# In the attention stage of a hybrid decoder step, ScalarE empties every second PSUM bank of transposed probabilities and VectorE the others

## The chip, the core and the metric

The kernel runs on one core of a Trainium2 chip. The metric is the time of one execution on the device in microseconds (us). The engines of a core that this text speaks of are TensorE (PE in the profile, PEld for its weight loads), VectorE (DVE), ScalarE (ACT), GpSimd (POOL) and SyncE (SP, which issues DMAs). Each works through its own list of instructions in order; they meet at semaphores.

## What is computed

One inference step of a two-layer decoder over a prompt of 1024 positions and eight sample sequences of 8 new positions each, model width 1024, all in float32. Layer 0 mixes tokens by retention and a gated recurrence; layer 1 by attention with 16 heads of 64 over three dilated windows. Both layers end in a SwiGLU block. The change lies in the attention of layer 1, whose prompt part is, for each pattern:

```
s = jnp.einsum('znqhd,znkhd->znhqk', qb, kc) * (Dh ** -0.5)
...
s = s - alibi_slopes()[:, None, None] * (d * diff)
s = jnp.where(valid[:, None], s, -jnp.inf)
m = jnp.max(s, axis=-1, keepdims=True)
p = jnp.exp(s - m)
den = jnp.sum(p, axis=-1)
o = jnp.einsum('znhqk,znkhd->znqhd', p, vc) / den.transpose(0, 1, 3, 2)[..., None]
```

The three patterns' results are then combined by their softmax denominators. The kernel folds the three patterns into one softmax over all earlier keys with a table of biases, which gives the same sum. The sample part does the same for 8 queries of each of eight sequences against a cache of 2048 keys and values, gathered by stride.

## The kernel before

Attention is done in 64 **steps**, one for each pair of heads and each block of 128 queries: step n has pair n // 8 and query block n % 8. The eight steps of a pair are called its first to eighth step; the eighth has eight key blocks (W = 1024), the first has one. A step's probabilities are worked on in three successive steps. For the pair's two heads (e = 0, 1) the stages are:

- `scores(n)` on TensorE (line 1833), into PSUM banks 0 to 3. VectorE adds the bias and takes the row extreme (line 2071, into `att_scores`), ScalarE does the exponentials in place with their sums (`probs(n, 0)` and `probs(n, 1)`, line 1982).
- In step n + 1 TensorE transposes these probabilities, 128x128 block by block (`turn`, line 1869), four blocks to a PSUM bank. Each bankful is a **unit** `("p", n, c)`, where c is its first block: 0, 4, 8, 12. An engine copies it to SBUF as `att_pt` (`take`, line 2036 on VectorE). A step of query block q has 2(q + 1) blocks, so one unit for q = 0 and 1, two for 2 and 3, three for 4 and 5, four for 6 and 7.
- In step n + 2 TensorE multiplies `att_pt` with the values (`pv`, line 1911) and spreads the inverse denominators (line 1915); ScalarE copies those out (`att_rden_rows`, line 2009), VectorE multiplies (`att_out`, line 2105).

All transposes share two PSUM banks (4 and 5) in turns: unit number g goes to bank g % 2, and `turn` first waits until unit g - 2 has been taken. `turns(n)` writes out by hand what units a step has. In steps up to 58 the sample work is woven in: three or four units of transposed cache keys (`"k"`, taken by ScalarE, `smp_kt`, line 1965) stand ahead of the "p" units in six of eight steps; in the other two stand units of queries and keys of the next pair ("qk") and of sample probabilities ("s"). A unit list of an eighth step is k, k, k, p0, p4, p8, p12. TensorE places units 0 and 1 first, then `pv` of step n - 2, then units 2 and 3, then the rest, with sample work between.

From step 59 on no cache keys are left, so the "p" units stand first: the **tail**. Step 61 has two units "out" ahead of them. Steps 64 and 65 have no scores of their own; step 65 has only `pv(63)`. After it comes the output projection (line 223), fed by `att_hi` (ScalarE, line 1815) and `att_lo` (VectorE, line 1819).

ScalarE's order within a step is set by these lines, where `mine` are the units that it takes:

```
for i in mine[0:2]:
    take(n, i)
...
if 0 <= n < NSLOT:
    probs(n, 0)
for i in mine[2:3]:
    take(n, i)
if 0 <= n < NSLOT:
    probs(n, 1)
for i in mine[3:]:
    take(n, i)
```

After them comes line 2009. At the end of step 61 ScalarE also splits a weight block (`w_hi`, line 205), and VectorE its rest (`w_lo`, line 209) at the end of step 62. VectorE does in each step: the scores' extremes (2071), a reciprocal (2076), its takes, then 2105.

Of the kernel before, what the change touches and what calls it, by code (L numbers as in the profile page):

```python
# [18 lines left out]
ACT = mybir.ActivationFunctionType  # L19
AX = mybir.AxisListType  # L20

P = 128
# [3 lines left out]
QT = SEQ // P  # L26
# [104 lines left out]
def build(nc, a):  # L131
# [349 lines left out]
    w = O_WORK  # L481
# [4 lines left out]
    w = O_WORK + 9 * TA  # L486
# [11 lines left out]
    w = O_X  # L498
# [22 lines left out]
    w = O_WORK  # L521
# [1153 lines left out]
    w = O_X  # L1675
# [5 lines left out]
    w = O_HL  # L1681
    BI = at("att_bias", w, [P, 2, 2, SEQ])
    PT = at("att_pt", w + 16384, [P, 2, 2 * QT, P])
# [12 lines left out]
    w = O_WORK  # L1696
# [48 lines left out]
    def turns(n):  # L1745
# [16 lines left out]
            units += [("s", b, z) for z in range(3)]  # L1762
        return units

    T0 = {}
    nt = 0
    for n in SLOTS:
# [3 lines left out]
    def last_turn(n, what, x):  # L1771

        g = T0[n] + max(i for i, u in enumerate(turns(n)) if u[0] == what and u[1] == x)
        return g % 2, g // 2 + 1

    def k_last(b, t):
        s = max(i for i in range(8) if K_AT[i] <= 2 * t + 1)
# [43 lines left out]
    def s9_pe(pe):  # L1821
# [78 lines left out]

        def pv(m):
            p, qb = divmod(m, QT)
            bank, count = last_turn(m + 1, "p", m)
            pe.wait_ge(t_out[bank], count)
            if qb == 0:
                pe.wait_ge(a_vl[p % 2], 16 * (p // 2 + 1))
            if m:
                pe.wait_ge(a_ox, m)
            for x in range(qb + 1):
                for e in range(2):  # L1910
                    pe.matmul(PS[e * DH:(e + 1) * DH, 6, 0:P], VN[p % 2][:, x, e * DH:(e + 1) * DH],  # L1911
                              PT[:, m % 2, e * (qb + 1) + x, :], start=(x == 0), stop=(x == qb), tile_position=(0, e * DH))
            pe.wait_ge(a_dg, m + 1)
            for e in range(2):
                mm = pe.matmul(PS[e * DH:(e + 1) * DH, 6, P:2 * P], ones[:, 0:DH], ADG[:, m % 2, e, :],
                               start=True, stop=True, tile_position=(0, e * DH))
            mm.then_inc(a_o, 1)
# [37 lines left out]
    def s9_act(act):  # L1955
        def take(n, i):
            what, x, c = turns(n)[i]
            g = T0[n] + i
            bank = PS[:, 4 + g % 2, :]
            act.wait_ge(t_in[g % 2], g // 2 + 1)  # L1960
            if what in ("qs", "ks"):
                act.activation((QTS, KTN)[what == "ks"][:, :, :].rearrange("p a w -> p (a w)"), bank,
                               ACT.Copy).then_inc(t_out[g % 2], 1)
            elif what == "k":
                act.activation(SKT[:, x % 2, 4 * c:4 * c + 4, :].rearrange("p a w -> p (a w)"), bank,  # L1965
                               ACT.Copy).then_inc(t_out[g % 2], 1)
            elif what == "qk":
                t = (QH, KH)[c // 2][x % 2]
                act.activation(t[:, (c % 2) * 512:(c % 2 + 1) * 512], bank, ACT.Copy).then_inc(q_hi, 1)
            else:  # L1970
                for e in range(2):
                    r = slice(e * DH, (e + 1) * DH)
                    dst = OX[r, :, S0 + 4 * x * DS:S0 + (4 * x + 4) * DS].rearrange("p k (b q) -> p b k q", q=DS)
                    src = bank[r, :].rearrange("p (b k e q) -> p b k e q", b=4, e=2, q=DS)[:, :, :, e, :]
                    op = act.activation(dst, src, ACT.Copy)
                op.then_inc(t_out[g % 2], 1)
# [8 lines left out]
        act.wait_ge(v_park, 16)  # L1985
        for n in SLOTS:
            b, s = sample_slot(n)
            mine = [i for i, u in enumerate(turns(n)) if u[0] not in ("p", "s")]
            for i in mine[0:2]:
                take(n, i)  # L1990
            if s == 6:
                act.wait_ge(b_mn, b + 1)
                act.activation(SS[:, :], SS[:, :], ACT.Exp, bias=NMN[:, 0:1], scale=-1.0,
                               accum_out=DNS[:, 0:1]).then_inc(b_p, 1)
# [8 lines that stand above are left out]
            if n == NSLOT + 1:  # L2003
                act.wait_ge(a_red, 2 * NSLOT)
                for k in range(3):
                    out1_hi(act, k)
            if 2 <= n:
                act.wait_ge(a_o, n - 1)
                act.activation(RS[:, n % 2, :], PS[:, 6, P:2 * P], ACT.Copy).then_inc(a_rc, 1)
            if n == NSLOT - LEAD + 1:  # L2010
                act.wait_ge(b_oc, DB)
                for e in range(2):
                    act.activation(ODUP[:, :, e, :], OALL[:, :].rearrange("p (b d) -> p b d", b=DB),
                                   ACT.Copy).then_inc(b_du, 1)
            if n == NSLOT - 3:
                split_hi(act, B_OUT1, B_OUT1 % RING)

    def s9_dve(dve):
# [41 lines left out]
        for n in SLOTS:  # L2060
# [19 lines left out]
                weigh(DB - 1)  # L2080
            for f in range(1, 5):
                for i in range(2 * f - 2, min(2 * f, len(units)) if f < 4 else len(units)):
                    if units[i][0] in ("qk", "p", "s"):
                        take(n, i)
                for t in SCORED.get((s, f), ()):
                    if t % 2:
# [296 lines left out]
```

## Time and profile before

| what | value |
|---|---|
| median of 3 runs | 2931.81 us (2929.42 to 2933.04) |
| profiled execution | 2934.2 us |
| its span from first to last instruction | 2932.4 us |
| PE busy | 2860.6 us, 98% of the span |
| DVE busy | 1358.0 us, 46% |
| ACT busy | 782.8 us, 27% |

The span is cut into engine busy times; the profiled execution's own time is 1.8 us above its span. Busy times are means over stages with different limits: the attention stage, from about 1562 to 2031 us of the span, has to be read by itself. A timeline row gives the start, the length, the engine, the line and operation, how many instructions were merged (x8), and in brackets the idle time of the engine ahead of it with what ended it.

### The profile page before, as it was taken

What the parts mean: (1) busy time and instruction counts of PE and PEld (TensorE: products, weight loads), DVE (VectorE), ACT (ScalarE), POOL (GpSimd) and SP (SyncE); (2) the same over time, 40 slices, a digit from 0 to 9 for tenths busy, and PEclk for the clock granted to TensorE, in tenths of its full rate; (3) what the DMA queues carried; (4) which work ended last, traced back from release to release, by engine and by line L of the source; (5) the groups of instructions that cost most, each with busy time, mean ns of one, the idle gap of its engine ahead of it and who ended that gap; (6) DMA issues with size and microseconds to landing.
All of it is one profiled execution on the core that took longest, in us unless ns stands there. A gap on an engine that the chain in (4) does not pass through costs nothing.

```text
span 2932.4 us, 47539 instructions
## 1 busy us (share of the span) xinstructions
PE 2860.6 (98%) x21361; PEld 2721.7 (93%) x21361; DVE 1358.0 (46%) x1756; ACT 782.8 (27%) x1238; POOL 117.4 (4%) x218
## 2 busy tenths in 40 slices
PE   7999999999999999999998999998999999999999
PEld 6999999999999999999996766777999999999999
DVE  5754544444444444745403555556444444444444
ACT  5443522111111111322215444444221111111111
POOL 1010000000000000000001111110000000000000
PEclk9999999999999999999999999999999999999999
DMA  5120211111111111222338667763111111111111
GB/s 190 44 67 18 105 58 44 44 44 44 44 44 44 44 44 44 105 75 90 102 122 275 203 202 248 247 196 123 58 44 44 44 44 44 44 44 44 44 44 61
DMA packets 126249, 253.80 MB, mean 87 GB/s; under 512 B 7585, under 2 KB 88693, under 8 KB 125536
## 3 DMA queue, kind: packets, MB, share of 16 engines
q1 hardware_dynamic: 112960, 189.29, 20.0%
q0 software_dynamic: 11776, 56.96, 5.7%
q10 hardware_dynamic: 1312, 4.52, 0.4%
q8 instruction: 169, 2.77, 0.4%
q14 instruction: 32, 0.26, 0.0%
HBM read 222.72 MB, written 28.02 MB: 86 GB/s over the span
## 4 chain that ended last, share of the span: by engine, by line
PE 91%; DVE 3%; ACT 3%; DMA 2%; SPq 1%; issue 1%; POOL 0%; ACTq 0%; POOLq 0%; DVEq 0%
PE psum L223 63%; PE psum L459 14%; PE psum L1854 3%; PE psum L1911 2%; PE psum L1869 2%; PE psum L1833 2%; PE psum L1882 1%; ACT smp_kt L1965 1%; DMA cache_tile<-in_cache_k 1%; SPq L1804 1%; DMA x_natural<-in_x_prompt 1%; PE psum L1935 0%; DVE att_pt L2036 0%; PE psum L568 0%; ACT att_scores L1982 0%
## 5 line engine op out<-in xcount | busy, mean ns | idle before, releaser
L223 PE MATMUL psum<-h_hi,w_hi 128*128 128x364 f32 (+1 forms) x2592 | 574.9, 330 | 6.5 <-DVE h_lo L289 5.6
L223 PE MATMUL psum<-h_lo,w_hi 128*128 128x364 f32 (+1 forms) x2592 | 571.6, 329 | 0.0
L223 PE MATMUL psum<-h_hi,w_lo 128*128 128x364 f32 (+1 forms) x2592 | 568.7, 328 | 0.0
L223 PEld LDWEIGHTS psum<-h_hi,w_hi 128*128 128x128 f32 x2592 | 448.6, 188 | 10.0 <-issue 6.8
L223 PEld LDWEIGHTS psum<-h_lo,w_hi 128*128 128x128 f32 x2592 | 449.1, 188 | 0.0
L223 PEld LDWEIGHTS psum<-h_hi,w_lo 128*128 128x128 f32 x2592 | 449.0, 188 | 0.0
L205 ACT ACTIVATE w_hi<-w_raw 128x2048 fp32r<-128x2048 f32 x96 | 183.5, 1912 | 665.5 <-PE psum L223 609.1
L459 PE MATMUL psum<-w_hi,h_hi 128*128 128x256 f32 (+1 forms) x1152 | 325.8, 283 | 0.0
L459 PE MATMUL psum<-w_hi,h_lo 128*128 128x256 f32 (+1 forms) x1152 | 323.6, 281 | 0.0
L459 PE MATMUL psum<-w_lo,h_hi 128*128 128x256 f32 (+1 forms) x1152 | 322.9, 280 | 0.0
L1473 DVE TENSOR_TENSOR x_res<-x_res,psum 128x1092 f32<-128x1092 f32 x176 | 227.3, 1292 | 200.3 <-PE psum L223 200.3
L209 DVE TENSOR_TENSOR w_lo<-w_raw,w_hi 128x2048 fp32r<-128x2048 f32 x96 | 219.6, 2288 | 63.2 <-ACT w_hi L205 49.0
L223 PE MATMUL psum<-ffn_hi,w_hi 128*128 128x364 f32 (+1 forms) x1056 | 233.3, 329 | 0.0
L223 PE MATMUL psum<-ffn_lo,w_hi 128*128 128x364 f32 (+1 forms) x1056 | 232.8, 328 | 0.0
L223 PE MATMUL psum<-ffn_hi,w_lo 128*128 128x364 f32 (+1 forms) x1056 | 232.7, 328 | 0.0
L459 PEld LDWEIGHTS psum<-w_hi,h_hi 128*128 128x128 f32 (+1 forms) x1152 | 215.1, 187 | 2.1 <-issue 1.2
L459 PEld LDWEIGHTS psum<-w_lo,h_hi 128*128 128x128 f32 (+1 forms) x1152 | 215.2, 187 | 0.0
L459 PEld LDWEIGHTS psum<-w_hi,h_lo 128*128 128x128 f32 (+1 forms) x1152 | 215.0, 187 | 0.0
L1450 DVE TENSOR_TENSOR ffn_t<-psum,rstd 128x1092 f32<-128x1092 f32 x44 | 57.0, 1296 | 296.7 <-PE psum L223 296.7
L1459 DVE TENSOR_TENSOR ffn_t<-psum,rstd 128x1092 f32<-128x1092 f32 x44 | 57.0, 1296 | 278.8 <-PE psum L223 278.6
L1422 ACT ACTIVATE ffn_hi<-ffn_t 128x1092 fp32r<-128x1092 f32 x44 | 49.2, 1118 | 507.6 <-DVE ffn_t L1461 507.6
L223 PEld LDWEIGHTS psum<-ffn_lo,w_hi 128*128 128x128 f32 x1056 | 183.0, 188 | 0.0
(309 smaller groups left out, 3192.5 us busy)
## 6 DMA issues: line engine op xcount, KB each, us to landing
cache_tile<-in_cache_k SPq DMA_DIRECT2D x64, 512.0 KB, 8.2
cache_tile<-in_cache_v SPq DMA_DIRECT2D x64, 512.0 KB, 5.6
w_raw<-in_w_ffn_gate SPq DMA_DIRECT2D x22, 1024.0 KB, 5.1
w_raw<-in_w_ffn_up SPq DMA_DIRECT2D x22, 1024.0 KB, 5.1
w_raw<-in_w_ffn_down SPq DMA_DIRECT2D x22, 1024.0 KB, 4.9
w_raw<-in_w_in_att SPq DMA_DIRECT2D x12, 1024.0 KB, 7.1
w_raw<-in_w_in_rec SPq DMA_DIRECT2D x10, 1024.0 KB, 5.0
park_x<-x_res POOLq DMA_DIRECT2D x2, 4368.0 KB, 14.0
```

Source lines behind the costliest of these rows:

```text
L205: act.activation(WHI[:, slot, :], RAW[:, :], ACT.Copy).then_inc(wh_done, 1)
L209: dve.tensor_tensor(WLO[:, slot, :], RAW[:, :], WHI[:, slot, :].bitcast(F32), ALU.subtract).then_inc(wl_done, 1)
L223: mm = pe.matmul(PS[:, bank + c, 0:n], st[:, slot, wc:wc + P], mv[:, k, c * CW:c * CW + n], start=(i < NCH), stop=(i >= 3 * NCH * nk - NCH))
L459: mm = pe.matmul(PS[0:n, bank, 0:BW], st[:, k, w:w + n], mv[:, slot, k * BW:(k + 1) * BW], start=(k == 0 and x == 0) if used is None else ...
L1422: act.activation(GH[:, par, f, :], TG[:, :], ACT.Copy).then_inc(fgh, 1)
L1450: i = dve.tensor_tensor(v3(TG[:, :]), PS[:, 0:3, 0:CW], r3, ALU.mult)
L1459: dve.tensor_tensor(v3(TG[:, :]), PS[:, 3:6, 0:CW], r3, ALU.mult).then_inc(fch, 1)
L1473: dve.tensor_tensor(x, x, PS[:, b0:b0 + 3, 0:CW], ALU.add).then_inc((a_out, b_out)[m % 2], 1)
L1833: mm = pe.matmul(PS[:, 2 * e + c // 512, 0:min(512, W - c)], q[p % 2][e * DH:(e + 1) * DH, qb * P:(qb + 1) * P], k[p % 2][e * DH:(e + 1) * ...
L1854: mm = pe.transpose(to[:, h * P:(h + 1) * P], TILE[j % 8][:, hp * P:(hp + 1) * P], ident[:, :])
L1869: mm = pe.transpose(to[:, (k - c) * P:(k - c + 1) * P], SX[x % 2][:, e, y * P:(y + 1) * P], ident[:, :])
L1911: pe.matmul(PS[e * DH:(e + 1) * DH, 6, 0:P], VN[p % 2][:, x, e * DH:(e + 1) * DH], PT[:, m % 2, e * (qb + 1) + x, :], start=(x == 0), stop ...
```

## The change

Of each step's "p" units, ScalarE now takes the second (c = 4) and the fourth (c = 12); VectorE keeps c = 0 and c = 8. TensorE's `pv` now waits for the last two units, since two engines may take them, where before it waited for the last one.

```
+    def by_act(unit):
+        what, x, c = unit
+        return c % 8 == 4 if what == "p" else what != "s"
...
+    def last_turns(n, what, x):
+
+        gs = [T0[n] + i for i, u in enumerate(turns(n)) if u[0] == what and u[1] == x]
+        return [(g % 2, g // 2 + 1) for g in gs[-2:]]
...
-            bank, count = last_turn(m + 1, "p", m)
-            pe.wait_ge(t_out[bank], count)
+            for bank, count in last_turns(m + 1, "p", m):
+                pe.wait_ge(t_out[bank], count)
...
+            elif what == "p":
+                k = min(4, 2 * (x % QT + 1) - c)
+                act.activation(PT[:, x % 2, c:c + k, :].rearrange("p a w -> p (a w)"), bank[:, 0:k * P],
+                               ACT.Copy).then_inc(t_out[g % 2], 1)
...
-            mine = [i for i, u in enumerate(turns(n)) if u[0] not in ("p", "s")]
+            mine = [i for i, u in enumerate(turns(n)) if by_act(u)]
...
-                    if units[i][0] in ("qk", "p", "s"):
+                    if units[i][0] == "qk" or not by_act(units[i]):
```

The first place is ScalarE in an eighth step (W = 1024), with the line of the exponentials at 1982 before and 1995 after. Before:

```order
L1965 ACTIVATE smp_kt<-psum 128x512 x2
L1982 ACTIVATE att_scores_176,att_den<-att_scores_176,att_max 128x1024
L1965 ACTIVATE smp_kt<-psum 128x512
L1982 ACTIVATE att_scores_176,att_den<-att_scores_176,att_max 128x1024
L2009 ACTIVATE att_rden_rows<-psum 128x128
```

With the change:

```order
L1974 ACTIVATE smp_kt<-psum 128x512 x2
L1995 ACTIVATE att_scores_176,att_den<-att_scores_176,att_max 128x1024
L1974 ACTIVATE smp_kt<-psum 128x512
L1995 ACTIVATE att_scores_176,att_den<-att_scores_176,att_max 128x1024
L1978 ACTIVATE att_pt<-psum 128x512
L1978 ACTIVATE att_pt<-psum 128x256
L2022 ACTIVATE att_rden_rows<-psum 128x128
```

Two copies have come in between the second exponential and the copy of the inverse denominators.

The second place is ScalarE in the tail, from step 61's exponentials (128x768) to the end of step 63. Before:

```order
L1982 ACTIVATE att_scores_176,att_den<-att_scores_176,att_max 128x768 x2
L2009 ACTIVATE att_rden_rows<-psum 128x128
L205 ACTIVATE w_hi<-w_raw 128x2048
L1982 ACTIVATE att_scores_175,att_den<-att_scores_175,att_max 128x896 x2
L2009 ACTIVATE att_rden_rows<-psum 128x128
L1982 ACTIVATE att_scores_176,att_den<-att_scores_176,att_max 128x1024 x2
L2009 ACTIVATE att_rden_rows<-psum 128x128 x2
```

With the change:

```order
L1995 ACTIVATE att_scores_176,att_den<-att_scores_176,att_max 128x768
L1978 ACTIVATE att_pt<-psum 128x512
L1995 ACTIVATE att_scores_176,att_den<-att_scores_176,att_max 128x768
L2022 ACTIVATE att_rden_rows<-psum 128x128
L205 ACTIVATE w_hi<-w_raw 128x2048
L1978 ACTIVATE att_pt<-psum 128x512
L1995 ACTIVATE att_scores_175,att_den<-att_scores_175,att_max 128x896 x2
L2022 ACTIVATE att_rden_rows<-psum 128x128
L1978 ACTIVATE att_pt<-psum 128x512
L1978 ACTIVATE att_pt<-psum 128x256
L1995 ACTIVATE att_scores_176,att_den<-att_scores_176,att_max 128x1024 x2
L2022 ACTIVATE att_rden_rows<-psum 128x128
```

Here the copies of `att_pt` stand among and ahead of the exponentials: one between the two of step 61, one ahead of those of step 62 (128x896), two ahead of those of step 63 (128x1024).

The third place is TensorE in step 63 after its scores: the transposes of its first two units (`att_scores_175`), `pv(61)`, and the transposes of the third and fourth unit, with the semaphores that each waits for. It stands in the same order before and after; this is the kernel with the change:

```order
L1878 MATMUL psum<-ident,att_scores_175 128x128 [waits att_probs,att_taken0]
L1878 MATMUL psum<-ident,att_scores_175 128x128 x3
L1878 MATMUL psum<-ident,att_scores_175 128x128 [waits att_probs,att_taken1]
L1878 MATMUL psum<-ident,att_scores_175 128x128 x3
L1920 MATMUL psum<-att_pt,att_v_186 64x128 [waits att_out_done,att_taken1,att_taken0]
L1920 MATMUL psum<-att_pt,att_v_186 64x128 x11
L1924 MATMUL psum<-att_diag,ones 64x128 [waits att_diag]
L1924 MATMUL psum<-att_diag,ones 64x128
L1878 MATMUL psum<-ident,att_scores_175 128x128 [waits att_probs,att_taken0]
L1878 MATMUL psum<-ident,att_scores_175 128x128 x3
L1878 MATMUL psum<-ident,att_scores_175 128x128 [waits att_probs,att_taken1]
L1878 MATMUL psum<-ident,att_scores_175 128x128
```

Before, the first five of these rows are

```order
L1869 MATMUL psum<-ident,att_scores_175 128x128 [waits att_probs,att_taken0]
L1869 MATMUL psum<-ident,att_scores_175 128x128 x3
L1869 MATMUL psum<-ident,att_scores_175 128x128 [waits att_probs,att_taken1]
L1869 MATMUL psum<-ident,att_scores_175 128x128 x3
L1911 MATMUL psum<-att_pt,att_v_186 64x128 [waits att_out_done,att_taken1]
```

Nothing moved on TensorE; only the wait of `pv` grew by one semaphore. The third unit of step 63 and the fourth (two blocks) are placed after `pv(61)`, on both kernels.

## Rows read from the trace of the kernel before

**Rows 1.** Windows: us, busy (x) of each engine, granted clock, DMA share.

```profile
1740.00:1800.00 60.00, 56.32 (x716) 41.82 (x716) 33.67 (x95) 29.39 (x70) 9.86 (x18) 1.00 0.70 222
...
2018.00:2022.00 4.00, 1.75 (x19) 1.09 (x16) 3.85 (x9) 2.55 (x5) 0.61 (x1) 1.00 0.87 302
...
2022.00:2026.00 4.00, 4.00 (x36) 3.67 (x37) 1.79 (x5) 0.00 (x0) 0.61 (x1) 0.57 0.15 52
```

**Rows 2.** Groups by form, attention stage: busy us, mean ns, idle before.

```profile
L2036 DVE COPY att_pt<-psum 128x512 f32<-128x512 f32 x128 | 86.0, 689 | 104.5 <-PE psum L1869 103.2
...
L2036 DVE COPY att_pt<-psum 128x256 f32<-128x256 f32 x32 | 13.5, 421 | 6.2 <-PE psum L1869 6.0
...
L1965 ACT ACTIVATE smp_kt<-psum 128x512 f32<-128x512 f32 x148 | 83.4, 595 | 154.8 <-PE psum L1854 154.4
...
L1982 ACT ACT_TABLE_LOAD x1 | 1.3, 1283 | 0.0
```

**Rows 3.** Line 1869, attention stage: TensorE's idle time before it (us, times).

```profile
  ACT smp_kt L1965: 22.9, 56
...
  DVE att_pt L2036: 14.6, 25
```

**Rows 4.** Timeline of the eighth step of a pair.

```profile
1736.74 1.14 ACT L1982 ACTIVATE att_scores<-att_scores,att_max 128x1024 f32<-128x1024 f32 x1
...
1737.15 1.09 PE L1869 MATMUL psum<-ident,att_scores 128*128 128x128 f32 x8
...
1737.85 1.65 DVE L2036 COPY att_pt<-psum 128x512 f32<-128x512 f32 x3
...
1737.87 0.27 ACT L2009 ACTIVATE att_rden_rows<-psum 128x128 f32<-128x128 f32 x1
...
1738.59 0.20 PEld L1869 LDWEIGHTS psum<-ident,att_scores 128*128 128x128 f32 x2 [0.58 <-DVE att_pt L2036]
```

**Rows 5.** Timeline of the steps after that.

```profile
1740.46 1.75 PE L1911 MATMUL psum<-att_pt,att_v 128*64 128x128 f32 x28
...
1757.34 0.20 PEld L1911 LDWEIGHTS psum<-att_pt,att_v 128*64 128x64 f32 x4 [0.17 <-issue]
```

**Rows 6.** Timeline of the tail, steps 60 to 62.

```profile
2000.90 1.09 PE L1869 MATMUL psum<-ident,att_scores 128*128 128x128 f32 x8 [0.34 <-DVE att_pt L2036]
...
2002.14 0.83 ACT L1982 ACTIVATE att_scores<-att_scores,att_max 128x640 f32<-128x640 f32 x1 [1.92 <-DVE att_max L2071]
...
2005.22 1.06 PE L1862 MATMUL psum<-ident,smp_out_twice 128*128 128x128 f32 x8 [0.95 <-ACT smp_out_twice L2013]
...
2009.61 1.91 ACT L205 ACTIVATE w_hi<-w_raw 128x2048 fp32r<-128x2048 f32 x1
...
2011.94 1.04 ACT L1982 ACTIVATE att_scores<-att_scores,att_max 128x896 f32<-128x896 f32 x1 [0.42 <-DVE att_max L2071]
...
2014.94 0.28 DVE L2105 TENSOR_TENSOR att_out<-psum,att_rden_rows 128x128 f32<-128x128 f32 x1
```

**Rows 7.** Timeline of the tail, steps 63 to 65.

```profile
2018.59 1.15 ACT L1982 ACTIVATE att_scores<-att_scores,att_max 128x1024 f32<-128x1024 f32 x1 [4.33 <-DVE att_max L2071]
...
2020.42 1.04 PE L1869 MATMUL psum<-ident,att_scores 128*128 128x128 f32 x6 [1.84 <-DVE att_pt L2036]
...
2021.87 1.79 PE L1869 MATMUL psum<-ident,att_scores 128*128 128x128 f32 x8 [0.41 <-DVE att_pt L2036]
...
2023.59 2.67 PE L1911 MATMUL psum<-att_pt,att_v 128*64 128x128 f32 x28
...
2026.40 1.09 PE L1869 MATMUL psum<-ident,att_scores 128*128 128x128 f32 x8
...
2028.73 1.97 PE L1911 MATMUL psum<-att_pt,att_v 128*64 128x128 f32 x32 [1.23 <-DVE att_out L2105]
```

**Rows 8.** Timeline of the output projection's start.

```profile
2036.27 3.10 ACT L1815 ACTIVATE att_hi<-att_out 128x1092 fp32r<-128x1092 f32 x3
...
2038.75 0.46 PEld L223 LDWEIGHTS psum<-att_hi,w_hi 128*128 128x128 f32 x3 [0.49 <-DVE att_lo L1819]
```

## The prediction

> **What bounds the kernel now.** I read the windows first, to see the attention stage by itself. In a middle stretch of it TensorE is busy 56.32 of 60 us, VectorE 33.67, ScalarE 29.39 [rows 1]: TensorE sets the pace and neither copying engine is full. What the change can win is therefore only idle time of TensorE that a copy of `att_pt` ends; what it can cost is idle time that it adds there. I next asked which waits end TensorE's idle time before the transposes of probabilities (line 1869). ScalarE's `smp_kt` ends 22.9 us of it, 56 times, VectorE's `att_pt` 14.6 us, 25 times, matmul and weight-load side added [rows 3]. Then I read the timeline of each kind of step. In the steps that carry cache keys, a transpose of probabilities waits for `att_pt` in one place only: the fourth unit (c = 12) of an eighth step waits for the bank of the second (c = 4), 0.58 us on the weight-load side [rows 4]. Seven eighth steps are of this kind (7, 15, ..., 55); the rest of the 14.6 us is in the tail. So two places have to be worked out: the eighth step, seven times, and the tail, once.
>
> **What moves.** Per pair the second units are one of 256 columns and five of 512, the fourth ones one of 256 and one of 512. That is 8 copies per pair, 64 in all, 48 of 512 columns and 16 of 256. VectorE is freed of 48 x 0.689 + 16 x 0.421 = 39.8 us [rows 2]. ScalarE's copy from PSUM of 512 columns takes 0.595 us [rows 2] and one of 128 columns 0.27 [rows 4]; on the line between them 256 columns take 0.38. ScalarE gains 48 x 0.595 + 16 x 0.38 = 34.6 us. Table loads are not added: copy and exponential already alternate on ScalarE with a single load in the stage [rows 2]. `pv` waits for one semaphore more in most steps. Today the first `pv` of a pair already waits for three (it adds the values' load), and its gap of 0.17 us [rows 5] is that of the others; I cost the wait at nothing (bounds 0 and 0.05 us x 50, 2.5 us).
>
> The Trainium skill, Perfetto Trace Analysis, Optimizing Scalar/DVE Operations, says that moving work to ScalarE may pay where VectorE is saturated. By that rule this change has nothing to win, since VectorE stands at 56% here.
>
> **The eighth step, with cache keys.** The first transposes of c = 4 are done some 0.65 us after 1737.15, and VectorE begins to copy them at 1737.85; the copy takes 0.69, and TensorE goes on at 1738.59, 0.05 us after its end [rows 4]. On ScalarE this copy stands behind the second exponential, which runs from 1736.74 for 1.14 us, to 1737.88 [rows 4]. So it runs from 1737.88 to 1738.47 and TensorE goes on at 1738.52: 0.07 us are saved, no more, and 7 x 0.07 = 0.5 us in all. If ScalarE were free in time, TensorE's own gap of 0.2 us would be left and 0.38 saved each time, 2.7 us: the lower bound. ScalarE's later row `att_rden_rows` (1737.87 before [rows 4]) moves behind both copies, to about 1739.4. VectorE's `att_out` and the `pv` behind it wait for it; that `pv` starts at 1740.46 [rows 5], one microsecond later than needed, which hides it. If that cover were gone, each 0.1 us uncovered in seven pairs would cost 0.7. In the third to seventh step the copy on ScalarE likewise stands behind the second exponential and ahead of the idle time before the next step's first cache keys (154.8 us of ScalarE's idle time end at `smp_kt` copies [rows 2], some 2 us at each step's first); nothing that TensorE waits for stands behind it. I take 0, bounds -2.7 and +2 us for the body without its 0.5.
>
> **The tail.** Here a step's "p" units are the first of `mine`, so ScalarE takes them ahead of its exponentials, and step by step falls behind. I follow it.
>
> Step 60: the transposes of both units run from 2000.90 for 1.09 us; the copy on ScalarE runs until about 2002.6, and the first exponential, 2002.14 before, starts 0.47 later [rows 6]. ScalarE stays late by that, and the "out" transposes, which waited for `smp_out_twice` at 2005.22 [rows 6], move by 0.47, with TensorE after them.
>
> Step 61: a copy stands between the two exponentials and waits 0.15 us for its transposes: 0.47 + 0.15 + 0.6 = 1.2 us late for the weight split, 2009.61 before and 1.91 long [rows 6]. It ends at 2012.7.
>
> Step 62: the copy of c = 4, 0.6 us, comes next; the exponentials, 2011.94 before [rows 6], start at 2013.3, 1.35 late. `att_rden_rows` follows them, and VectorE's `att_out` after it, before at 2014.94 [rows 6], at about 2015.66: 0.72 late. Behind it on VectorE stand the weight's rest and step 63's extremes, and behind these the take of step 63's first unit.
>
> Step 63: the third unit waits for that take and starts at 2020.42 + 0.73 = 2021.15; third and fourth are done 0.87 later, the 0.18 us that the fourth waited for VectorE in the 1.04 being gone [rows 7]: 2022.02. Only now can ScalarE copy the fourth unit, since it stands **ahead of the exponentials of step 63**: until 2022.44. Then two exponentials of 1.15 us [rows 7], with 0.1 us for the sum read between and behind: 2024.84, where before they had been over at about 2020.9. Step 64's first transposes read them. They start at 2024.89 instead of 2021.87 [rows 7]: **+3.0 us**.
>
> Step 64: before, the transposes took 1.79 us and `pv(62)` 2.67 [rows 7]; eight transposes at 2026.40 take 1.09 [rows 7] and 28 such matmuls elsewhere 1.75 [rows 5]. The granted clock was 0.57 between 2022 and 2026 (1.2 GHz for most of it), after a stretch of 4 us in which TensorE was busy 1.75 [rows 1]. With the change that stretch is emptier still, so I take the low clock to hold over the same work: 0 more. Bounds: full clock, -(0.70 + 0.92) = -1.6; the low clock over the next transposes and `pv(63)` too, +0.7 + 0.9 = +1.6, and over the first microseconds of the projection, some +1 more.
>
> The Trainium skill, TensorE: Matmul & The Clock Gate, HAM oscillation, holds that idle gaps on TensorE bring the low clock. By that rule a second gap after the first (2.9 us of idle time between 2022.0 and 2024.9) speaks for the bound above, not for the one below; the row before it agrees (0.57 after a gap of 1.84 us).
>
> End of step 64: the fourth unit is now copied by ScalarE (1.1 us after the transposes start, 0.6 long) ahead of `att_rden_rows`, and VectorE's `att_out` comes some 0.1 us later relative to the transposes; `pv(63)`, which waited 1.23 us for it at 2028.73 [rows 7], moves by that: **+0.1**. ScalarE's first three `att_hi`, which had filled the time of these transposes, begin 1.7 us later, so the chain `att_hi`, `att_lo`, `att_out(63)`, `att_hi` runs 1.3 us behind. Its last link was just in time: TensorE waited 0.49 us (0.19 of it felt) for the sixth `att_lo`, behind `att_hi` at 2036.27 [rows 8]. **+1.25 us** (bounds 0 and 1.7).
>
> **Sum.** -0.5 + 3.0 + 0 + 0.1 + 1.25 = +3.9 us. On the profiled execution's own 2934.2 us this gives 2938.1; that execution lies 2.4 us above the median of the runs, 2931.8, so the predicted time is 2935.7.
>
> **Rivals.** (1) *A gain*: VectorE's lighter queue lets extremes and `att_out` come sooner and TensorE loses its waits for `att_pt`. For it speak the 25 waits; against it that ScalarE is at its exponentials whenever a second unit is ready. It would give -2.7 in the body and up to -3 in the tail (VectorE is busy 3.85 of 4 us there [rows 1]): 2926 us. It decides if ScalarE's queue had 0.3 us to spare at the second units. Chance 0.06. (2) *A wash*: the tail's delay of the exponentials is made up, because VectorE reaches step 63 sooner by two copies (1.3 us) and `pv(62)` is not held: +3.0 shrinks to 1 or 2 and with full clock the sum is near 0: 2932 us. Chance 0.17. (3) *The stall feeds on itself*, slower by over 0.2%: the low clock lasts over `pv(63)` and the projection's start (+1.6 + 1), or the second copy of an eighth or first step holds `att_rden_rows` long enough that `pv` waits 0.3 us in 14 steps (+4). It decides once 2 us come on top of 3.9. It gives +6.5 to +8: 2939 us. Chance 0.21. That only part of the units move is ruled out by the order: 64 copies stand on ScalarE. The forecast itself has 0.56.
>
> **How the numbers follow.** A measurement of this kernel can tell about 0.2%, 5.9 us, from no change. +3.9 is within it, and so is case 2. Range: from case 2's lower side, -1 us, to case 3's upper side, +8.4: 2930.8 to 2940.2. Faster by more: most of case 1, 0.05. Slower by more: 0.22. Same: 0.73.
>
> **What would show it.** Right: in eighth steps the transposes' wait turns from `att_pt` of VectorE to `att_pt` of ScalarE and stays near 0.5 us; the distance from one pair's eighth step to the next pair's stays as it is; in step 64 TensorE stands idle near 2.9 us for `att_scores` of ScalarE, at about 2025; a wait of 1 to 1.5 us before line 223. Wrong: that distance moving by over 0.1 us, the exponentials of step 63 over before 2023, or a low granted clock that reaches into line 223.

## The result

The kernel with the change takes **2937.22 us** (median of 18 runs, 2932.25 to 2943.62), the kernel before 2930.87 us (18 runs beside them, 2926.13 to 2938.24). The ratio is 1.0017 with a 95% interval of 1.0010 to 1.0024, so 2.9 to 7.0 us more, 5.0 in the middle (the two medians lie 6.35 us apart). The middle is within the 0.2%, 5.9 us, called "the same" above, though the interval leaves no doubt that it is a loss. The profiled execution after has a span of 2939.8 us.

The page of the kernel after, busy time of each engine:

```profile
PE 2864.3 (97%) x21361; PEld 2725.1 (93%) x21361; DVE 1325.2 (45%) x1692; ACT 815.5 (28%) x1302; POOL 117.3 (4%) x218
```

VectorE has 32.8 us less than before, ScalarE 32.7 us more: the work moved. The page counts overlapping edges of instructions once (three copies in [rows 4] take 1.65 us together, 1.80 apart by [rows 2]), so VectorE's busy time fell by less than the 39.8 us of its 64 copies.

Line 1878 (1869 before), attention stage of the kernel after; TensorE's idle time before it by releaser (us, times), which answers to [rows 3]:

```profile
  ACT smp_kt L1974: 22.1, 54
...
  DVE att_pt L2049: 6.1, 7
...
  ACT att_pt L1978: 5.4, 14
...
  ACT att_scores L1995: 2.8, 1
```

The 14.6 us that ended at VectorE's `att_pt` are 6.1 now. 6.5 of them, 14 entries, lay in the seven eighth steps; they are the 5.4 us that end at ScalarE's `att_pt` now. The other 2.0 went in the tail. And there is a new entry: one wait of 2.8 us for `att_scores`, in step 64, in place of one for `att_pt`.

The eighth step after, which answers to [rows 4]:

```profile
1737.18 0.59 ACT L1978 ACTIVATE att_pt<-psum 128x512 f32<-128x512 f32 x1
...
1737.81 0.20 PEld L1878 LDWEIGHTS psum<-ident,att_scores 128*128 128x128 f32 x2 [0.50 <-ACT att_pt L1978]
...
1738.29 0.39 ACT L1978 ACTIVATE att_pt<-psum 128x256 f32<-128x256 f32 x1 [0.53 <-PE psum L1878]
```

The fourth unit still waits, for the same bank, only 0.50 us in place of 0.58, in all seven eighth steps.

The tail after, steps 60 to 64, in order of time. The rows answer to [rows 6] and [rows 7]:

```profile
2004.06 1.06 PE L1878 MATMUL psum<-ident,att_scores 128*128 128x128 f32 x8
...
2008.72 1.07 PE L1871 MATMUL psum<-ident,smp_out_twice 128*128 128x128 f32 x8 [1.32 <-ACT smp_out_twice L2026]
...
2013.66 1.91 ACT L205 ACTIVATE w_hi<-w_raw 128x2048 fp32r<-128x2048 f32 x1
...
2015.94 1.05 ACT L1995 ACTIVATE att_scores<-att_scores,att_max 128x896 f32<-128x896 f32 x1
...
2017.82 0.69 DVE L2049 COPY att_pt<-psum 128x512 f32<-128x512 f32 x1 [0.75 <-PE psum L1878]
...
2018.43 0.28 DVE L2118 TENSOR_TENSOR att_out<-psum,att_rden_rows 128x128 f32<-128x128 f32 x1
2018.63 2.28 DVE L209 TENSOR_TENSOR w_lo<-w_raw,w_hi 128x2048 fp32r<-128x2048 f32 x1
...
2021.97 0.08 DVE L2084 DVE_READ_ACCUMULATOR2_ANT att_max<- 128x1 f32 x1
...
2023.92 0.87 PE L1878 MATMUL psum<-ident,att_scores 128*128 128x128 f32 x6 [1.84 <-DVE att_pt L2049]
...
2024.83 0.38 ACT L1978 ACTIVATE att_pt<-psum 128x256 f32<-128x256 f32 x1 [3.79 <-PE psum L1878]
2025.11 1.14 ACT L1995 ACTIVATE att_scores<-att_scores,att_max 128x1024 f32<-128x1024 f32 x1
...
2026.24 1.14 ACT L1995 ACTIVATE att_scores<-att_scores,att_max 128x1024 f32<-128x1024 f32 x1
...
2027.61 1.94 PE L1878 MATMUL psum<-ident,att_scores 128*128 128x128 f32 x8 [2.82 <-ACT att_scores L1995]
...
2029.48 3.17 PE L1920 MATMUL psum<-att_pt,att_v 128*64 128x128 f32 x28
...
2032.80 1.09 PE L1878 MATMUL psum<-ident,att_scores 128*128 128x128 f32 x8
...
2035.16 1.97 PE L1920 MATMUL psum<-att_pt,att_v 128*64 128x128 f32 x32 [1.27 <-DVE att_out L2118]
...
2042.17 0.46 PEld L223 LDWEIGHTS psum<-att_hi,w_hi 128*128 128x128 f32 x3 [0.45 <-DVE att_lo L1828]
...
2045.98 0.46 PEld L223 LDWEIGHTS psum<-att_hi,w_hi 128*128 128x128 f32 x3 [0.87 <-DVE att_lo L1828]
```

Look at the two rows of ScalarE at 2024.83 and 2025.11. The extreme of the first head was read out at 2021.97 (to 2022.05), so the first exponential could have started then. It starts 3.1 us later, because the copy of the fourth unit stands ahead of it in ScalarE's queue, and that copy has to wait (3.79 us idle) for TensorE's transposes. Then TensorE in its turn waits 2.82 us for both exponentials.

A yardstick for the tail: the time from step 60's first transposes to the matmuls behind the sixth `att_lo`. The profile has no wait for a transfer between them. Before it is 2038.75 - 2000.90 = 37.85 us [rows 6, 8], after it is 2045.98 - 2004.06 = 41.92, **4.07 more**. The rows divide it: 0.34 at the "out" transposes (4.32 us behind step 60's first before [rows 6], 4.66 now), 0 from there to step 63's third unit (15.20 in both), 2.24 in front of step 64 (1.45 us behind the third unit before [rows 7], 3.69 now), 0.66 by the low clock, 0.03 at `pv(63)`, 0.80 at the sixth `att_lo`. Behind it both kernels run alike to the end (893.65 us before, 893.82 after).

The spans themselves cannot be compared term by term. The distance from one eighth step to the next differed by up to 2.2 us between two executions (58.1 us before and 60.3 after at the same place), through waits for cache tiles; there it was 60.5 us in experiment 10, which has VectorE's copies as before, and 58.5 us in experiment 11, which has the whole change. The difference of the two spans, 7.4 us, holds such pieces beside the 4.07.

### The profile page after: what moved, and what is told of

Read it like the earlier page. It is cut to its first block, busy times and chain, and to the rows that moved or that the text cites. A ratio compares the mean times of both kernels' runs of the same rounds, so it can differ in the third digit from the quotient of the medians.

```text
span 2939.8 us, 47539 instructions
## 1 busy us (share of the span) xinstructions
PE 2864.3 (97%) x21361; PEld 2725.1 (93%) x21361; DVE 1325.2 (45%) x1692; ACT 815.5 (28%) x1302; POOL 117.3 (4%) x218
## 4 chain that ended last, share of the span: by engine, by line
PE 90%; ACT 3%; DVE 3%; DMA 2%; SPq 1%; issue 1%; POOL 0%; ACTq 0%; POOLq 0%; DVEq 0%
PE psum L223 63%; PE psum L459 14%; PE psum L1863 3%; PE psum L1920 2%; PE psum L1842 2%; PE psum L1878 2%; DMA cache_tile<-in_cache_k 1%; PE psum L1891 1%; ACT smp_kt L1974 1%; ACT att_scores L1995 1%; SPq L1813 1%; DMA x_natural<-in_x_prompt 1%; PE psum L568 0%; PE psum L1924 0%; PE psum L1867 0%
## 5 line engine op out<-in xcount | busy, mean ns | idle before, releaser
L1450 DVE TENSOR_TENSOR ffn_t<-psum,rstd 128x1092 f32<-128x1092 f32 x44 | 57.0, 1296 | 296.8 <-PE psum L223 296.8
L223 PEld LDWEIGHTS psum<-ffn_hi,w_hi 128*128 128x128 f32 x1056 | 183.0, 188 | 0.0
```

Source lines behind the costliest of these rows:

```text
L223: mm = pe.matmul(PS[:, bank + c, 0:n], st[:, slot, wc:wc + P], mv[:, k, c * CW:c * CW + n], start=(i < NCH), stop=(i >= 3 * NCH * nk - NCH))
L1450: i = dve.tensor_tensor(v3(TG[:, :]), PS[:, 0:3, 0:CW], r3, ALU.mult)
```

## The experiments

The theory: the copy of step 63's fourth unit, which stands ahead of the exponentials, makes the stall, and the copy of step 64's fourth unit delays the projection. The rivals: ScalarE's lateness piles up over the tail until it shows in step 64; the body or the second semaphore takes the time; the low clock does. All kernels are measured beside the kernel before.

**1 and 2: one half of the change at a time.** The first keeps it for x < 58 alone, the second for x >= 58 alone, with that comparison in the same line (the diff is that of the first, against the kernel with the change; x is the step whose probabilities the unit holds).

```
-        return c % 8 == 4 if what == "p" else what != "s"
+        if what == "p":
+            return c % 8 == 4 and x < 58
+        return what != "s"
```

> Only the units of steps up to 58 (those with cache keys) go to ScalarE as in the change; the tail is as before. My theory (all the cost is in the tail): the fourth unit of an eighth step waits 0.50 us on the weight-load side instead of 0.58, seven times, the stretch from step 60's first transposes to the sixth att_lo of the projection lasts 37.85 us as before, and the time is that of before less 0.5 us. Rival (the body pays too, by later att_rden_rows or the wider wait of pv): the distance between eighth steps grows by 0.1 to 0.3 us, +1 to +2 us in the time.

> Only the tail's units (steps 59 to 64) go to ScalarE; the body is as before. My theory: the stretch from step 60's first transposes to the sixth att_lo lasts 41.9 us, as with the whole change (4.1 more than before), with an idle time near 2.8 us ahead of step 64's first transposes; time +4 to +5 us. Rival (the body pays a part): less than +3 us, and a shorter stretch.

Measured: the body alone 2932.4 us (11 runs) beside 2932.45 (33 runs), ratio 0.9998 [0.9989, 1.0007]; the tail alone 2938.55, ratio 1.0021 [1.0012, 1.0029]. The loss is all in the tail. The eighth steps of the first wait 0.51 us for ScalarE, those of the second 0.58 or 0.59 for VectorE; yardstick 37.47 and 41.10, where 37.85 and 41.9 were expected. What they miss by is the low clock, which was shorter in both: without it they are 36.21 and 39.68, against 36.23 and 39.65 of before and of the whole change.

**3: one unit alone.** Only step 63's fourth unit goes to ScalarE, one copy of 0.39 us in the whole kernel. In `by_act` a "p" unit now has

```
+            return (x, c) == (62, 12)
```

> One single copy of 64 goes to ScalarE: the fourth unit (c = 12, two blocks, 0.38 us) that is turned in step 63. My theory, that the copy's place ahead of the exponentials of step 63 is the cost: these exponentials end at about 2024.5 on the clock of before, step 64's first transposes start 2.2 to 2.5 us later than before after an idle time near 2.5 us, and the whole stretch from step 60 on grows by 2.3 to 3.5 us. Rival (the load on ScalarE, 5 copies in five steps, is the cost): one copy of 0.38 us costs 0.4 us at most.

Measured: 2936.56 us (11 runs), ratio 1.0010 [1.0002, 1.0019]: 2.9 us by the ratio, 4.1 us in the medians. Timeline of this kernel, steps 63 and 64:

```profile
2021.44 1.03 PE L1880 MATMUL psum<-ident,att_scores 128*128 128x128 f32 x6 [1.84 <-DVE att_pt L2051]
...
2022.51 0.39 ACT L1980 ACTIVATE att_pt<-psum 128x256 f32<-128x256 f32 x1 [7.24 <-PE psum L1880]
2022.79 1.14 ACT L1997 ACTIVATE att_scores<-att_scores,att_max 128x1024 f32<-128x1024 f32 x1
...
2023.92 1.14 ACT L1997 ACTIVATE att_scores<-att_scores,att_max 128x1024 f32<-128x1024 f32 x1
...
2025.29 1.51 PE L1880 MATMUL psum<-ident,att_scores 128*128 128x128 f32 x6 [2.82 <-ACT att_scores L1997]
```

The stall is there in full with ScalarE idle for 7.24 us ahead of the copy: nothing is late on ScalarE, so the rival of a lateness that piles up falls. The copy waits for data, and the exponentials wait behind it. Step 64 starts 3.85 us behind the third unit, 2.40 more than before.

**4: the whole change, with that copy placed behind the exponentials.**

```
+            if n == NSLOT - 1:
+                mine = mine[0:1] + [None, None] + mine[1:]
             for i in mine[0:2]:
-                take(n, i)
+                if i is not None:
+                    take(n, i)
...
             for i in mine[2:3]:
-                take(n, i)
+                if i is not None:
+                    take(n, i)
```

> The whole change, but in step 63 ScalarE takes the fourth unit after the two exponentials instead of ahead of them; nothing else moves. My theory: no idle time for the exponentials ahead of step 64's first transposes (they start some 0.4 us after those of before, relative to step 60), the low clock still follows the first idle time of 1.84 us but over less work, and the stretch from step 60 to the sixth att_lo is 39.0 to 39.6 us, of which 0.3 from steps 60 and 61 and 0.8 from the end of step 64: 2.2 to 3 us better than the change, +1.5 us against before. Rival (load on ScalarE): as slow as the change, 41.9 us.

Measured: 2932.84 us (11 runs), ratio 1.0003 [0.9994, 1.0012]. Timeline:

```profile
2020.89 1.15 ACT L1995 ACTIVATE att_scores<-att_scores,att_max 128x1024 f32<-128x1024 f32 x1 [1.06 <-DVE att_max L2088]
...
2022.04 1.14 ACT L1995 ACTIVATE att_scores<-att_scores,att_max 128x1024 f32<-128x1024 f32 x1
...
2023.63 0.38 ACT L1978 ACTIVATE att_pt<-psum 128x256 f32<-128x256 f32 x1 [0.35 <-PE psum L1878]
...
2024.16 1.09 PE L1878 MATMUL psum<-ident,att_scores 128*128 128x128 f32 x8 [0.56 <-DVE att_pt L2053]
```

All 64 copies are still on ScalarE, only one stands elsewhere. The exponentials start when the extremes come, and step 64 follows the third unit by 1.44 us as before. Of the ratio of 1.0017 there is 1.0003 left. The yardstick is 37.42, where 39.0 to 39.6 was expected: the expectation had the low clock in it, and this execution ran at full clock. Of the 4.50 us below the whole change, 2.23 are then the stall and 2.27 the low clock. What stays against before at full clock (36.23) is the 0.37 by the "out" transposes and the 0.8 at the projection.

**5: the other fourth unit alone**, step 64's, one copy of 0.60 us; in `by_act`:

```
+            return (x, c) == (63, 12)
```

> One single copy goes to ScalarE: the fourth unit (c = 12, four blocks) that is turned in step 64, which then stands ahead of att_rden_rows and of the first three att_hi. My theory, that it is this copy that cost 0.8 us at the projection's start: nothing before it moves, pv(63) starts 0 to 0.1 us later relative to step 64's third unit (2.33 us before), and TensorE's wait for the sixth att_lo grows from 0.49 to about 0.87 on the weight-load side, with a new wait of 0.45 for the third or fourth, 0.8 us in all. Rival (those 0.8 us come from the general lag of ScalarE in the tail): no new wait, below 0.2 us.

Measured: 2934.38 us (10 runs) beside 2932.73 (33 runs), ratio 1.0007 [0.9997, 1.0017]; the time does not tell it from no change, the trace does: weight loads of the projection,

```profile
2032.68 0.47 PEld L223 LDWEIGHTS psum<-att_hi,w_hi 128*128 128x128 f32 x3 [0.45 <-DVE att_lo L1830]
...
2036.49 0.46 PEld L223 LDWEIGHTS psum<-att_hi,w_hi 128*128 128x128 f32 x3 [0.87 <-DVE att_lo L1830]
```

The two waits of the whole change, 0.45 and 0.87, are here and nothing else of it; from the third unit's transposes of step 64 to the sixth `att_lo` 13.18 us, before 12.35. That is the 0.8, and it belongs to this copy: in experiment 3, with the stall but without this copy, the wait was 0.49 as before.

**6 and 7: the clock.** Matmuls that nobody reads, identity transposes into an unused PSUM bank, fill TensorE's idle time: in the kernel with the change 12 in step 63's gap and 20 ahead of step 64, in the kernel before 12 in step 63's gap.

```
+            for i in range(20 if n == NSLOT else 0):
+                pe.transpose(PS[:, 7, 0:P], ident[:, :], ident[:, :])
...
+                for i in range(12 if (n, f) == (NSLOT - 1, 2) else 0):
+                    pe.transpose(PS[:, 7, 0:P], ident[:, :], ident[:, :])
```

> The changed kernel, with 12 transposes of the identity matrix that nobody reads put into TensorE's idle time of 1.84 us in step 63 and 20 more into that of 2.82 us at the start of step 64 (extra work, written to a PSUM bank that is free by then). If idle time of TensorE is what brings the low clock there: granted clock 1.00 from 2020 to 2036, step 64's eight transposes take 1.09 us and pv(62) 1.75 (1.94 and 3.17 without), and the stretch from step 60's first transposes to the sixth att_lo falls from 41.9 to 39.7 to 40.3 us, although TensorE has more to do. If the clock falls for another reason (the time of the span, what the DMAs do): no change, or longer by the filling. The stall itself stays: the exponentials end where they ended.

> The kernel before with only the 12 unread transposes in the idle time of step 63 (extra work). If idle time brings the low clock: step 64 runs at full clock, the stretch from step 60 to the sixth att_lo is 36.2 to 36.4 us instead of 37.85, time -1 to -1.6 us. Otherwise 37.9 or more.

Measured: with the change and filled 2936.64 us (10 runs), ratio 1.0013 [1.0003, 1.0022]; before and filled 2931.61 (10 runs), ratio 0.9998 [0.9988, 1.0008]. Timeline of TensorE with the change and the filling:

```profile
2026.23 0.88 PE L1878 MATMUL psum<-ident,att_scores 128*128 128x128 f32 x6 [0.39 <-DVE att_pt L2053]
...
2029.93 1.06 PE L1878 MATMUL psum<-ident,att_scores 128*128 128x128 f32 x8 [0.64 <-ACT att_scores L1999]
...
2030.92 1.75 PE L1920 MATMUL psum<-att_pt,att_v 128*64 128x128 f32 x28
```

and its windows over step 64, with the granted clock behind the engines:

```profile
2028.00:2030.00 2.00, 1.36 (x13) 1.15 (x12) 0.02 (x1) 1.95 (x5) 0.00 (x0) 1.00 0.23 81
2030.00:2032.00 2.00, 2.00 (x28) 1.83 (x30) 1.04 (x3) 0.60 (x1) 0.62 (x1) 1.00 0.01 5
```

against the same stretch of the kernel with the change alone:

```profile
2026.00:2028.00 2.00, 0.39 (x2) 0.42 (x3) 0.34 (x2) 1.63 (x5) 0.00 (x0) 0.50 0.12 41
2028.00:2030.00 2.00, 2.00 (x14) 1.67 (x14) 0.72 (x2) 0.41 (x1) 0.61 (x1) 0.50 0.02 7
```

The clock stays at 1.00 (2.4 GHz) and `pv(62)` takes 1.75 us, not 3.17. The stall stays: 3.70 us from the third unit to step 64. So the low clock is a separate term (2.27 us in the trace), and the times of 6 and of the change alone can't be told apart. This is one profile against four with the stall and without filling. Experiment 7 says little by itself: its clock stayed at 1.00 (yardstick 36.23), but so it did in three of five profiles with the same gap and nothing in it.

**8: a version that takes only what looked like a gain**: the body's change, and VectorE's `w_lo` moved one step later, since it stands ahead of step 63's extremes and of the take that the third unit waits for.

```
-            if n == NSLOT - 2:
+            if n == NSLOT - 1:
```

> The change up to step 58 only, and the rest of the first output weight block (w_lo, 2.28 us on VectorE) computed at the end of step 63 instead of step 62, so that step 63's extremes no longer stand behind it. What the runs point to: in step 63 TensorE's idle time of 1.84 us shrinks to 0.4 to 0.5, step 64 starts 1.4 us sooner and keeps the full clock; VectorE has idle time in step 64 for the 2.28 us. Stretch from step 60 to the sixth att_lo 34.9 to 35.6 us (37.85 before), time -2.5 to -3.5 us against before. Rival: VectorE's weight rest now delays the takes of step 64 and nothing is won, 37.5 us or more.

Measured: 2931.84 us (11 runs), ratio 0.9997 [0.9989, 1.0006]. That is 0.9 us in the medians where 2.5 to 3.5 was expected. The yardstick is 35.10 us as expected, but against 36.2 of the kernel before at full clock, and not 37.85: a gain of 1.1 us in the trace that the times don't resolve.

**9 to 11: the semaphore, and `w_lo` by itself.** The kernel before with the wait of `pv` for two units; the kernel before with `w_lo` one step later; the whole change with `w_lo` one step later.

```
-            bank, count = last_turn(m + 1, "p", m)
-            pe.wait_ge(t_out[bank], count)
+            for bank, count in last_turns(m + 1, "p", m):
+                pe.wait_ge(t_out[bank], count)
```

> VectorE copies all the probability units, as before; only the wait of `pv` for the last two units in place of the last one is kept. Theory (the extra semaphore costs nothing, since the second to last unit has been taken long before the last one): 2932.7 us, no difference to before; `pv` after a long row of matmuls still begins with a gap of 0.17 us; the stretch from step 60's first transposes to the sixth att_lo stays at 36.2 us (at full clock) to 37.9 (with the low clock in step 64). Rival (each extra semaphore costs 0.05 us): +2.5 us over 50 steps and gaps of 0.22 us.

> The kernel before, with VectorE's part of the weight split (w_lo) moved from the end of step 62 to the end of step 63, and nothing else. Theory (w_lo stands ahead of step 63's extremes and of the take that the third unit waits for): the idle time before the third unit, 1.84 us, shrinks to about 0.4, and the stretch from step 60's first transposes to the sixth att_lo goes from 36.2 (full clock) to 35.1 us, as in the kernel with the body's change and this move; so that kernel's 1.1 us belong to this move. Rival (they belong to the body's change): the stretch stays at 36.2 us or more. By time: 2931.6 us, not to be told from before.

> The whole change, with w_lo moved from the end of step 62 to the end of step 63. Theory (the exponentials of step 63 hang on the transposes of its fourth unit, so whatever brings these earlier brings step 64 earlier by as much): the third unit of step 63 starts about 1.1 to 1.4 us sooner after the out turns, at 13.9 in place of 15.2 us behind them, and step 64's first transposes still start 3.7 us after it with 2.8 us idle; stretch 40.5 us with the low clock, 38.5 without. Rival (the exponentials are late from a delay of ScalarE that piles up since step 60, not from the fourth unit): step 64's first transposes stay 18.9 us behind the out turns, and the stretch stays at 39.7 to 41.9 us.

Measured, beside 2931.58 us (27 runs): 2931.08, ratio 0.9994 [0.9985, 1.0002]; 2930.44, 0.9995 [0.9986, 1.0004]; 2935.44, 1.0011 [1.0002, 1.0020] (11 runs each). The semaphore costs nothing that can be told: the interval ends at +0.6 us, the yardstick is 36.23, and `pv` still begins after 0.17 us. Timeline of TensorE in the kernel of `w_lo` alone and in that of the whole change with it:

```profile
2017.30 1.04 PE L1869 MATMUL psum<-ident,att_scores 128*128 128x128 f32 x6 [0.43 <-DVE att_pt L2036]
...
2018.74 1.09 PE L1869 MATMUL psum<-ident,att_scores 128*128 128x128 f32 x8 [0.40 <-DVE att_pt L2036]
...
2022.13 1.26 PE L1869 MATMUL psum<-ident,att_scores 128*128 128x128 f32 x8 [0.40 <-DVE att_pt L2036]
```

```profile
2016.37 0.87 PE L1878 MATMUL psum<-ident,att_scores 128*128 128x128 f32 x6 [0.44 <-DVE att_pt L2049]
...
2020.06 1.94 PE L1878 MATMUL psum<-ident,att_scores 128*128 128x128 f32 x8 [2.82 <-ACT att_scores L1995]
```

As expected, in both the wait of 1.84 us ahead of the third unit is 0.43 or 0.44. In the second the stall of 2.82 us has moved forward with the third unit and is as long as ever. Step 64 starts 17.49 us behind the "out" transposes, 1.40 sooner than with the change alone, so it hangs on the fourth unit's transposes and not on a lateness of ScalarE from before them. (The yardstick of this one, 41.07, is longer than the 40.5 expected for the low clock, and without it 38.7 where 38.5 was expected.)

All kernels by the yardstick, in us. "Low clock" is what the first transposes of step 64 take over 1.09 us and `pv(62)` over 1.75; the last column but one is the yardstick without it.

| kernel | yardstick | low clock | without it | third unit to step 64 |
|---|---|---|---|---|
| before | 37.85 | 1.62 | 36.23 | 1.45 |
| with the change | 41.92 | 2.27 | 39.65 | 3.69 |
| 1 body | 37.47 | 1.26 | 36.21 | 1.44 |
| 2 tail | 41.10 | 1.42 | 39.68 | 3.70 |
| 3 unit (62, 12) alone | 41.21 | 2.36 | 38.85 | 3.85 |
| 4 that copy behind | 37.42 | 0 | 37.42 | 1.44 |
| 5 unit (63, 12) alone | 37.06 | 0 | 37.06 | 1.44 |
| 6 change, filled | 39.66 | 0 | 39.66 | 3.70 |
| 7 before, filled | 36.23 | 0 | 36.23 | 1.44 |
| 8 body, `w_lo` later | 35.10 | 0 | 35.10 | 1.44 |
| 9 two waits | 36.23 | 0 | 36.23 | 1.44 |
| 10 before, `w_lo` later | 35.29 | 0 | 35.29 | 1.44 |
| 11 change, `w_lo` later | 41.07 | 2.36 | 38.71 | 3.69 |

Four kernels whose tail should be that of before (before, 1, 7, 9) agree within 0.02 us. `w_lo` one step later gives 0.94 us with the old tail (36.23 to 35.29) and 0.94 with the change (39.65 to 38.71), where 1.1 was expected: the third unit of step 63 comes 1.41 us sooner, and 0.47 are lost again at step 64's third unit (the row at 2022.13), which now waits for a VectorE copy behind `w_lo`. Experiment 8 lies 0.19 below experiment 10, but 0.18 of that stands at the stretch's own start (4.14 us from step 60's first transposes to the "out" ones, 4.32 in experiment 10), where TensorE had no wait of 0.34 us. Experiment 1 has the same body and 4.33, so this is not a gain of the body's change.

## Why the prediction was right

The median lies 1.5 us above the predicted 2935.7 and within the range. The increase is the better test, since the kernel before came out at 2930.87 beside it and not at the 2931.8 that the sum started from: 5.0 us by the ratio, where 3.9 was forecast. Its steps, one by one:

- **The eighth step, -0.5**: right. 0.58 or 0.59 went to 0.50 or 0.51 in all seven, the copy standing behind the second exponential as worked out. The body alone gave no time that could be told (0.9998).
- **The body otherwise, 0, and the wait for two semaphores, 0**: right, by experiments 1 and 9.
- **Step 64's first unit, +3.0**: the mechanism was right, the size too large. It measured 0.34 + 2.24 = 2.58 us. The stall itself was priced right, at 2.29 us (3.74 from the third unit to step 64, for 1.45); the rest, 0.73, was the delay carried to the third unit, and that was too much. The term had 0.47 carried from step 60, and 0.34 came. It then let the carried delay grow to 0.73 by step 63, and nothing was added: step 63's third unit came 15.20 us behind the "out" transposes in both kernels. The reason is in the rows at 2015.94 and 2018.43: against the carried 3.50 us of the trace the exponentials of step 62 are 0.50 late, not 0.88, and VectorE's `att_out`, which moved by 3.49 (2014.94 [rows 6] to 2018.43), stands behind VectorE's own copy of step 62's third unit (the row at 2017.82, which waited for TensorE), not behind ScalarE's `att_rden_rows`.
- **The low clock, 0**: mis-sized. It cost 0.66 more in the profiled execution (1.94 for 1.79 us, 3.17 for 2.67, and 0.01 between). The bound of 1.6 above was not reached there: step 64's third unit took 1.09 us and `pv(63)` 1.97 as before, and from 2034 us on the granted clock was 1.00, line 223 included.
- **`pv(63)`, +0.1**: 0.03 (the wait is 1.27 for 1.23).
- **The projection, +1.25**: 0.80. The cause was right, ScalarE's copy ahead of the first `att_hi`, as experiment 5 shows; the slack behind it was set too small. Before and after:

```profile
2026.70 3.11 ACT L1815 ACTIVATE att_hi<-att_out 128x1092 fp32r<-128x1092 f32 x3
...
2028.30 0.28 DVE L2105 TENSOR_TENSOR att_out<-psum,att_rden_rows 128x128 f32<-128x128 f32 x1
2028.50 3.70 DVE L1819 TENSOR_TENSOR att_lo<-att_out,att_hi 128x1092 fp32r<-128x1092 f32 x3
```

```profile
2034.58 3.12 ACT L1824 ACTIVATE att_hi<-att_out 128x1092 fp32r<-128x1092 f32 x3
...
2035.73 3.71 DVE L1828 TENSOR_TENSOR att_lo<-att_out,att_hi 128x1092 fp32r<-128x1092 f32 x3 [0.71 <-ACT att_hi L1824]
```

  Counted from step 64's third unit (2026.40 and 2032.80), the first `att_hi` comes 1.48 us later (1.78 for 0.30), the first `att_lo` only 0.83 (2.93 for 2.10), since before it stood behind VectorE's `att_out` and not behind `att_hi`. The chain keeps these 0.83 to its end, where 1.3 had been reckoned.

The sum of the measured terms is -0.5 + 4.07 = +3.6, predicted +3.9, and the ratio gives +5.0 (2.9 to 7.0). That the two sums lie so near is in part luck: the two terms that were too large by 0.42 and 0.45 are offset by the 0.66 of low clock that was put at nothing. The rest could be the clock, which one execution can't tell: the sum was made against a profiled execution of before that had the low clock (1.62 us in step 64). Of five kernels with the old gap of 1.84 us in front of the third unit and 1.44 or 1.45 behind, unfilled (before, 1, 4, 5, 9), two had it and three ran at full clock. Of four with the stall (the change, 2, 3, 11) all had it, at 1.42 to 2.36 us. If most executions of before have none, the change costs -0.5 + 3.42 (39.65 - 36.23) + 2.27 = 5.2 us. Nine profiles are few for that. The mean granted clock of whole executions (10 to 33 runs of each kernel) points the same way, weakly: 0.9947 to 0.9952 in three of the four kernels with the unfilled stall, but 0.9960 in experiment 11, against 0.9957 to 0.9969 in all without it. Such a mean doesn't say which stretch it comes from. It stays a likely reading.

Of the signs named ahead, those for right came: the eighth steps' wait ends at ScalarE's `att_pt`, TensorE stands idle 2.82 us for `att_scores` ahead of step 64, and two waits of 0.45 and 0.87 us stand before line 223. One sign for wrong was badly chosen. The distance between eighth steps did move by over 0.1 us, by up to 2.2, but it moves as much between kernels whose copies in the body are the same, so it tells nothing.

Of the rivals, the gain didn't come, since ScalarE was at its exponentials when the second units were ready. The wash was wrong on its main point: VectorE did not reach step 63 sooner, as the wait of 1.84 us stayed what it was. The stall that feeds on itself, by a low clock over `pv(63)` and the projection, was not seen in any trace; nor did `pv` of the next step wait behind an eighth step, where its gap is 0.17 us as before.

The Trainium skill, TensorE: Matmul & The Clock Gate, HAM oscillation, holds that idle gaps bring the low clock. The traces agree for the stall (low in four of four, and at 1.00 in the one where it was filled), and leave open when the shorter gap does (two of five).

## What to carry to other kernels

An offload is judged by its place in the new engine's queue, not by its length. One copy of 0.39 us cost 2.4 us of TensorE's time, since it waited for later data ahead of two exponentials that were ready, and it cost nothing behind them. So look at each moved instruction for what it waits for and what stands behind it, above all at the ends of a loop, where the order of the steady state no longer fits. And where executions scatter by more than the effect, compare a stretch between two rows that no transfer disturbs.

## What the runs showed of the hardware

- The same idle time of TensorE led to different clocks. After 1.84 and 0.41 us of idle time the kernel before had 0.57 over the next 4 us [rows 1], and the kernel of experiment 5 had 1.00:

```profile
2018.00:2022.00 4.00, 2.64 (x24) 2.06 (x26) 3.70 (x11) 1.67 (x5) 1.23 (x2) 1.00 0.71 233
2022.00:2026.00 4.00, 2.73 (x40) 2.35 (x38) 1.36 (x3) 1.56 (x3) 0.00 (x0) 1.00 0.05 19
```

- At the low level (1.2 GHz) eight transposes took 1.79 to 1.97 us for 1.09, and 28 matmuls of `pv` up to 3.26 for 1.75.
- Transposes that nobody reads, placed in the gaps, went with a clock of 1.00 in both kernels that had them (three of the five unfilled ones with the short gap had 1.00 too), without delaying the work behind them by more than 0.01 us by the yardstick (39.66 for 39.65, 36.23 for 36.23).
